# Moving three quarters of an attention output projection into the steps of the last attention group

## The chip, the cores and the metric

The kernel runs on one core of a Trainium2 chip. The metric is the time of one execution in microseconds (us), measured on the device; a kernel's time is the median of its runs. The engines are PE (TensorE, matrix products), ACT (ScalarE), DVE (VectorE), POOL (GpSimd) and SP, which here only starts DMA transfers. Each takes its instructions in program order, and waits between engines are semaphore counts.

## What is computed

A decoder trunk of two layers on 512 positions and a model width of 1024: sparse attention (NSA), a SwiGLU feed-forward (FFN), a Mamba-2 mixer, a second FFN. The part at issue is the end of the attention and the start of the first FFN:

```python
    gates = jax.nn.sigmoid(g.astype(jnp.float32)).reshape(B, S, G, HP, 3, 1)
    o = (gates[..., 0, :] * o_c + gates[..., 1, :] * o_s + gates[..., 2, :] * o_w).astype(h.dtype)
    return o.reshape(B, S, NSA_Q_WIDTH) @ w_out
...
        h = h + mix.astype(h.dtype)
        h = h + swiglu(rms_norm(h, ffn_norm_w[i]), ffn_w_gate[i], ffn_w_up[i], ffn_w_down[i]).astype(h.dtype)
```

## The kernel before

Activations are kept transposed: `xT` is 128 partitions x 8 tiles (`KT`) x 512 positions. Every dense product is done in three matmuls, because each fp32 operand is split into a rounded high part and a rest: high x high, high x rest, rest x high (`split_product`). Weights arrive in chunks of 1 MB (128 x 2048 floats) through a ring of two slots: SP loads chunk n into `wraw[n % 2]`, ACT copies it into `wh` (`split_hi`, 128x2048), DVE writes the rest into `wl` (`split_lo`), and PE multiplies. SP may load chunk n+2 once `lo_done` says that chunk n is split; `split_hi` of chunk n waits until PE has finished chunk n-2 (`products`, two counts for each chunk).

Attention is done in 4 groups of 4 heads, each group in 18 steps `k`. Each engine has its own program for a step, in this order:

- PE: for k = 8, 12, 16 first `pv` of a head (18 matmuls); then `qk(k)` (scores of a head h = k // 4 and a block of 128 queries i = k % 4, so that the width is (i+1) x 128), small steps for the compressed attention at k = 0, 1, 5, then `pT(k-2)` (2(i+1) transposes of the probabilities).
- DVE: `maxima(k)` of the scores, `normalize(k-1)` of the exponentials, compressed attention at k = 1 and 3, and at k = 14 `o_rest(0)`; the last, `o_rest(1)`, follows after step 17.
- ACT: `exps(k-1)`, `pT_copy(k-2)` from PSUM, and `o_copy`.

`maxima(k)` waits for `qk(k)`, `exps` for the maxima, `normalize` for the exponentials, `pT` for `normalize`, `pT_copy` for `pT`, and `pv` for the copies of four blocks. The first three groups also carry the q/k/v projection of the next group (`project`, 8 matmuls in each of the steps 0 to 11, all into PSUM bank 7, which ACT empties). They also split the next two weight chunks in steps 14 and 15. The last group carries nothing besides attention. Heads come out two at a time as one tile of `xo` (high) and `xol` (rest), 8 tiles in all; tiles 6 and 7 are those of the last group.

Then follows `residual("nsa_out")`: four chunks of the output weights, each of 256 columns by all 8 input tiles. PE makes 8 output tiles of 24 matmuls into banks 0 to 3 in turn. For each pair of tiles DVE adds the two banks to `xT` (loaded again from memory by ACT's queue) and makes `xl` (`x_lo`), and ACT makes the squares for the norm (`square`) and `xh` (`x_hi`), POOL adds the squares up. Three `split_hi`/`split_lo` go between the pairs. The FFN begins with `pe.wait_ge(evac, t0)`: all 8 tiles must have been added to `xT`. Its first chunk needs `xh` and `xl` tile by tile; between its two output tiles stand `column_sums`, for which POOL must be done.

Of the kernel before, what the change touches and what calls it, by code (L numbers as in the profile page):

```python
# [31 lines left out]
P = 128  # L32
# [48 lines left out]
def chunk_plan():  # L81

    at, n = {}, 0
    for name, count in (("kv_cmp", 2), ("gates", 1), ("qkv", 8), ("nsa_out", 4), ("up0", 2 * FT // 2),
                        ("down0", 12), ("xbc", 12), ("dt", 1), ("z", 8), ("ssm_out", 8),
                        ("up1", 2 * FT // 2), ("down1", 12)):
        at[name] = n
        n += count
    return at, n


CHUNK, NCHUNKS = chunk_plan()

EVAC, _t = {}, 0
for _name, _count in (("kv_cmp", 4), ("gates", 1), ("qkv", 16), ("nsa_out", 8), ("up0", FT), ("down0", 8),
# [8 lines left out]
def trunk(nc, wstream, xT_in, cols_in, rows_in, pos_in, cw1_in, cw2_in, ident_in, tri_in, cmask_in, out):  # L104
    with ExitStack() as ctx:
# [3 lines left out]
        def sem(name):  # L109
            return ctx.enter_context(nc.semaphore(name))  # L110


        class Region:
# [4 lines left out]
            def take(self, name, shape, dt=F32):  # L118
# [110 lines left out]
        a = Region(arena_at)  # L229
        yl = a.take("yl", [P, TT, 16, P], F32R)  # L230
        a = Region(act_at)
        yh = a.take("yh", [P, TT, 16, P], F32R)
        assert a.end <= res_at
        a = Region(scratch_at)
# [16 lines left out]
            sem, ("masks_cast", "square_sum_zeroed", "squares_done", "square_sum_done", "colsum_done",  # L251
                  "mean_square_done", "rms_rstd_done", "diag_done", "rstd_broadcast_done"))
        xh_done, xl_done, vz_zeroed, vz_done = map(sem, ("xh_done", "xl_done", "vz_zeroed", "vz_done"))
        gate_in, gate_done, hh_done, hl_done = map(sem, ("gate_normed", "gate_done", "hidden_hi_done", "hidden_lo_done"))
        vec, pool_self = map(sem, ("vector_step", "pool_step"))
        (mhalf_set, kvT, tb_act, tb_vec, tbT_done, rows_mm, rows_copied, hid_mm, hid_done, cmp_mm, kc_sq, kc_mean, kc_rstd, kcn_done, kcT, kc_hi, kc_padded, kc_staged,
# [41 lines left out]

        Q4 = "p (h d) -> p h d"

        RES = {"nsa_out": [8], "ssm_out": [8, 8], "down0": [8, 8, 6], "down1": [8, 8, 6]}
        NORM = {"nsa_out": 1, "down0": 2, "ssm_out": 3}

        EARLY = ("nsa_out", "down0")
        NORMCOL = [COL_MIX, COL_FFN, COL_MIX + KT, COL_FFN + KT]

        block = ctx.enter_context(nc.Block())
# [2 lines left out]
        @block.sync  # L310
        def _(sp):
            sp.dma_start(cols[:, :], cols_in).then_inc(cols_landed, 16)
            for k in range(4):
                sp.dma_start(xT[:, 2 * k:2 * k + 2, :], xT_in[:, 2 * k:2 * k + 2, :]).then_inc(x_landed[k], 16)
                if k == 0:
                    sp.dma_start(wraw[:, 0, :], wstream[0]).then_inc(landed[0], 16)
            sp.dma_start(wraw[:, 1, :], wstream[1]).then_inc(landed[1], 16)
            sp.dma_start(tri[:, :, :], tri_in).then_inc(params_landed, 16)
            sp.dma_start(ident[:, :], ident_in).then_inc(params_landed, 16)
            sp.dma_start(rows[:, :], rows_in).then_inc(params_landed, 16)  # L320
            sp.dma_start(posi[:, :], pos_in).then_inc(rest_landed, 16)
            sp.dma_start(cmask[:, :, :, :], cmask_in).then_inc(rest_landed, 16)
            sp.dma_start(cw1[:, :, :, :], cw1_in).then_inc(cw_landed, 16)
            sp.dma_start(cw2[:, :, :, :], cw2_in).then_inc(cw_landed, 16)
            with sp.Fori(1, NCHUNKS // 2) as i:
                for k in range(2):

                    sp.wait_ge(lo_done, 2 * i + (k - 1))
                    sp.dma_start(wraw[:, k, :], wstream[bass.ds(2 * i + k, 1)].rearrange("a p n -> p (a n)")
                                 ).then_inc(landed[k], 16)  # L330
            for t in range(KT):
                sp.wait_ge(evac, EVAC["down1"] + t + 1)
                sp.dma_start(out[:, t, :], xT[:, t, :]).then_inc(out_stored, 16)
            sp.wait_ge(out_stored, 16 * KT)
# [3 lines left out]
        def _(pe):  # L338
# [180 lines left out]
            def group(g, more):  # L519
# [68 lines left out]
                def project(part):  # L588
# [12 lines left out]
                    if third == 2:  # L601
                        ins.then_inc(products, 1)

                for k in range(18):
                    if k in (8, 12, 16):
                        pv((k - 8) // 4)
                    if k < 16:
                        qk(k)
                    if k == 0:
                        cmp_scoresT()  # L610
                    if k == 1:
                        cmp_scores()
                    if k == 5:
                        cmp_transposes()
                    if k >= 2:
                        pT(k - 2)
                    if more and k < 12:
                        project(k)
                    if more and k == 16:
                        pe.wait_ge(evac, g * 4 + (t0 + 4))  # L620
                        qk_transposes(g + 1, (0, 1, 2), lambda h: (h - 1) % 8)
                    if more and k == 17:
                        qk_transposes(g + 1, (3, 4), lambda h: h - 1)
                        pe.wait_ge(qkT_lo, g * 6 + 7)
                        qk_transposes(g + 1, (5,), lambda h: 7)
# [26 lines left out]
                pe.wait_ge(qkT_lo, g * 6 + 12)  # L652
            group(GROUPS - 1, False)
            pe.wait_ge(o_lo, 2 * GROUPS)
            residual("nsa_out", lambda kt: (xo[:, kt, :], xol[:, kt, :]))
            ffn("up0", "down0", 1)


# [135 lines left out]
        def _(act):  # L794
# [27 lines left out]
            def residual(name):  # L822
                ks, n0, t0 = RES[name], CHUNK[name], EVAC[name]
                per = 2 * len(ks)
                ahead = name in ("nsa_out", "ssm_out")

                def turn(i, shift):

                    for p in range(2):
                        for q in range(len(ks)):  # L830
                            n = n0 + p * len(ks) + q + 1 + shift * per
                            if n < NCHUNKS and not ahead:
                                split_hi(n, i, per)
                            if ahead and q < len(ks) - 1:
                                split_hi(n + 1)
                        if name in NORM:
                            for m in range(2):
                                t = 2 * p + m + 4 * shift
                                square(t, NORM[name], i, 4, t0)
                                if name in EARLY:  # L840
                                    x_hi(NORM[name], t if i is None else i * 4 + t)
                        if ahead and n + 1 <= n0 + 2 * per:
                            split_hi(n + 1)
                if n0 + 2 * per < NCHUNKS and not ahead:
                    with act.Fori(0, 2) as i:
                        turn(i, 0)
                else:
                    turn(None, 0)
                    turn(None, 1)
                if name in NORM and name not in EARLY:  # L850
                    for kt in range(KT):
                        x_hi(NORM[name], kt)

# [85 lines left out]
            def group(g, more):  # L939
# [18 lines left out]
                def o_copy(pr):  # L958
                    act.wait_ge(pv_done, g * 4 + 2 * (pr + 1))
                    A(xo[:, bass.ds(g * 2 + pr, 1), :].rearrange("p a n -> p (a n)"), ps[:, 6, :], ACT.Copy  # L960
                      ).then_inc(o_hi, 1)

                for k in range(18):
# [23 lines left out]
                    if more and k in (14, 15):  # L987
                        act.wait_ge(products, g * 4 + 2 * (n0 + 4))
                        split_hi(n0 + 4 + k - 14, g, 2)
                o_copy(1)  # L990

            transposed_hi(0, (0, 1, 2), lambda h: h)
# [4 lines left out]
            A(Bc[:, 0, :], ps[:, 6, 3 * P:4 * P], ACT.Copy).then_inc(kc_hi, 1)  # L997
            with act.Fori(0, GROUPS - 1) as g:
                group(g, True)
            group(GROUPS - 1, False)  # L1000
            act.wait_ge(o_lo, 2 * GROUPS)
            act.dma_start(xT[:, :, :], xT_in).then_inc(x_again, 16)
            residual("nsa_out")
            ffn("up0", "down0", 1)


# [106 lines left out]
        def _(dve):  # L1113
# [35 lines left out]
            def residual(name):  # L1149
                ks, n0, t0 = RES[name], CHUNK[name], EVAC[name]  # L1150
                per = 2 * len(ks)
                ahead = name in ("nsa_out", "ssm_out")

                def turn(i, shift):
                    for p in range(2):
                        for q in range(len(ks)):
                            n = n0 + p * len(ks) + q + 1 + shift * per
                            if n < NCHUNKS and not ahead:
                                split_lo(n, i, per)
                            if ahead and q < len(ks) - 1:  # L1160
                                split_lo(n + 1)
# [9 lines left out]
                                x_lo(NORM[name], t if i is None else i * 4 + t)  # L1171
                        if ahead and n + 1 <= n0 + 2 * per:
                            split_lo(n + 1)
                if n0 + 2 * per < NCHUNKS and not ahead:
# [131 lines left out]
            def group(g, more):  # L1306
# [56 lines left out]
                for k in range(18):  # L1363
# [21 lines left out]
                        transposed_lo(g + 1, (3, 4, 5), lambda h: h - 1 if h < 5 else 7)  # L1385
                    if more and k in (14, 15):
                        split_lo(n0 + 4 + k - 14, g, 2)
                o_rest(1)

            split_lo(5)  # L1390
# [37 lines left out]
                group(g, True)  # L1428
            V.leave(GROUPS - 1, DVE_GROUP_STEPS)
            group(GROUPS - 1, False)  # L1430
            dve.wait_ge(x_again, 16)
            residual("nsa_out")
            ffn("up0", "down0", 1)


# [370 lines left out]
```

## Time and profile before

| what | value |
|---|---|
| median of 3 runs | 1648.72 us (1648.58 to 1653.01) |
| span of the profiled execution | 1649.7 us |
| PE busy | 1561.1 us, 95% of the span |
| DVE busy | 867.8 us, 53% |
| ACT busy | 631.6 us, 38% |
| POOL busy | 258.2 us, 16% |
| mean granted PE clock | 0.975 of 2.4 GHz |

The span goes from the first to the last instruction of one profiled execution. The profiled execution is not among the three timed runs and has no time of its own beside its span; the span is 1.0 us above the median of the runs. Busy time counts matrix products from their start to a modelled end, so two that follow each other overlap: a product of 128x512 is shown as 0.39 us long, but the next starts 0.23 us after it. Start to start is therefore what a product costs.

### The profile page before, as it was taken

How to read it: one execution, taken by the hardware profiler on the slowest of the kernel's cores; microseconds unless marked ns; L12 is line 12 of the kernel's file. 1: busy time of each engine (PE TensorE's matmuls, PEld its weight loads, DVE VectorE, ACT ScalarE, POOL GpSimd, SP SyncE). 2: the span in 40 equal slices, each digit the busy share in tenths (PEclk: the TensorE clock that was granted, in tenths of full speed). 3: DMA queues.
4: the chain of work that ended last, by engine and by line, in shares of the span. 5: the costliest groups of instructions: out<-in, count | busy, mean ns of one | idle time of the engine just before them, and what ended most of it. 6: DMA issues, size and time to landing. Idle time of an engine off the chain costs nothing.

```text
span 1649.7 us, 19940 instructions
## 1 busy us (share of the span) xinstructions
PE 1561.1 (95%) x7085; PEld 1223.5 (74%) x7085; DVE 867.8 (53%) x1265; ACT 631.6 (38%) x895; POOL 258.2 (16%) x288
## 2 busy tenths in 40 slices
PE   5989999988999999999999999998799999999999
PEld 4766666654778888878888877666587788887887
DVE  4555767574444444432377766778732544444222
ACT  4444555554334433422233353444222434433111
POOL 4133131400200000000000015666311000000000
PEclk9989999989999999999999999999799999999999
DMA  7200101010222222223222221110022222222222
GB/s 302 77 26 1 52 0 51 0 51 1 102 91 87 102 102 102 102 80 124 102 77 103 85 94 51 52 51 27 24 77 103 77 102 80 98 102 102 103 102 76
DMA packets 19196, 129.44 MB, mean 78 GB/s; under 512 B 2256, under 2 KB 2896, under 8 KB 4560
## 3 DMA queue, kind: packets, MB, share of 16 engines
q1 hardware_dynamic: 19008, 126.75, 21.4%
q10 hardware_dynamic: 144, 2.10, 0.4%
q8 instruction: 28, 0.46, 0.1%
q14 instruction: 16, 0.13, 0.0%
HBM read 126.74 MB, written 2.10 MB: 78 GB/s over the span
## 4 chain that ended last, share of the span: by engine, by line
PE 83%; issue 5%; DVE 5%; POOL 5%; ACT 2%; DVEq 0%; POOLq 0%; ACTq 0%
PE ps L343 21%; PE ps L344 21%; PE ps L345 21%; PE ps L582 4%; PE ps L599 3%; PE ps L747 2%; PE ps L565 2%; POOL Lx L1697 2%; PE ps L579 1%; PE ps L530 1%; POOL sqacc L1623 1%; DVE Pm L1355 1%; PE ps L719 1%; PE ps L531 1%; PE ps L777 1%
## 5 line engine op out<-in xcount | busy, mean ns | idle before, releaser
L1125 DVE TENSOR_TENSOR wl<-wraw,wh 128x2048 fp32r<-128x2048 f32 x112 | 264.7, 2364 | 273.9 <-ACT wh L802 273.8
L343 PE MATMUL ps<-xh,wh 128*128 128x512 f32 (+2 forms) x912 | 358.9, 393 | 6.1 <-DVE xl L1135 3.4
L345 PE MATMUL ps<-xh,wl 128*128 128x512 f32 (+2 forms) x912 | 355.9, 390 | 0.0
L344 PE MATMUL ps<-xl,wh 128*128 128x512 f32 (+2 forms) x912 | 355.9, 390 | 0.0
L802 ACT ACTIVATE wh<-wraw 128x2048 fp32r<-128x2048 f32 x112 | 213.9, 1910 | 186.3 <-PE ps L345 176.6
L343 PEld LDWEIGHTS ps<-xh,wh 128*128 128x128 f32 (+2 forms) x912 | 170.4, 187 | 44.3 <-issue 4.5
L345 PEld LDWEIGHTS ps<-xh,wl 128*128 128x128 f32 (+2 forms) x912 | 170.5, 187 | 37.2
L344 PEld LDWEIGHTS ps<-xl,wh 128*128 128x128 f32 (+2 forms) x912 | 170.6, 187 | 36.8 <-issue 0.7
L343 PE MATMUL ps<-hh,wh 128*128 128x512 f32 x352 | 138.0, 392 | 4.0 <-DVE hid L1205 4.0
L345 PE MATMUL ps<-hh,wl 128*128 128x512 f32 x352 | 137.6, 391 | 0.0
L344 PE MATMUL ps<-hl,wh 128*128 128x512 f32 x352 | 137.6, 391 | 0.0
L1623 POOL TENSOR_TENSOR sqacc<-sqacc,sq 128x512 f32<-128x512 f32 x32 | 44.2, 1381 | 482.0 <-ACT sq L811 481.0
L864 ACT ACTIVATE hh<-hid 128x512 f32 x44 | 27.8, 632 | 188.4 <-DVE hid L1205 188.4
L1342 DVE TENSOR_REDUCE sm<-ps 128x2 f32<-128x256 f32 (+1 forms) x64 | 52.5, 821 | 70.1 <-PE ps L532 70.1
L343 PEld LDWEIGHTS ps<-hh,wh 128*128 128x128 f32 x352 | 66.4, 189 | 18.7 <-DVE hid L1205 4.9
L955 ACT ACTIVATE PT<-ps 128x256 f32<-128x256 f32 (+1 forms) x64 | 45.1, 704 | 91.5 <-PE ps L565 91.5
L344 PEld LDWEIGHTS ps<-hl,wh 128*128 128x128 f32 x352 | 66.5, 189 | 13.8
L345 PEld LDWEIGHTS ps<-hh,wl 128*128 128x128 f32 x352 | 66.5, 189 | 13.8
L947 ACT ACTIVATE Pm<-ps,sm 128x128 f32<-128x128 f32 (+3 forms) x128 | 66.3, 527 | 23.6 <-DVE sm L1344 23.4
L582 PE MATMUL ps<-PT,vst 128*64 128x512 f32 (+3 forms) x256 | 74.0, 443 | 0.0
L582 PEld LDWEIGHTS ps<-PT,vst 128*64 128x64 f32 x256 | 35.2, 141 | 48.7 <-issue 43.6
L1168 DVE TENSOR_TENSOR xT<-ps,xT 128x512 f32<-128x512 f32 (+1 forms) x32 | 22.1, 690 | 85.7 <-PE ps L345 77.9
(257 smaller groups left out, 2560.1 us busy)
## 6 DMA issues: line engine op xcount, KB each, us to landing
wraw<-wstream SPq DMA_DIRECT2D x112, 1024.0 KB, 4.8
cw<-cw_in SPq DMA_DIRECT2D x1, 4096.0 KB, 18.3
xT<-xT_in SPq DMA_DIRECT2D x4, 512.0 KB, 9.0
xT<-xT_in ACTq DMA_DIRECT2D x1, 2048.0 KB, 7.8
out<-xT SPq DMA_DIRECT2D x8, 256.0 KB, 6.6
rows<-rows_in SPq DMA_DIRECT2D x1, 276.0 KB, 11.1
tri<-tri_in SPq DMA_DIRECT2D x1, 192.0 KB, 9.7
cmask<-cmask_in SPq DMA_DIRECT2D x1, 128.0 KB, 10.5
```

The lines of the kernel that those rows point to most:

```text
L343: mm(o, wa[0], xa[0], start=start, stop=False)
L344: mm(o, wa[0], xa[1], start=False, stop=False)
L345: return mm(o, wa[1], xa[0], start=False, stop=stop)
L565: ins = pe.transpose(ps[:, 4 + b, j * P:(j + 1) * P], Pm[:, s % 2, b, j * P:(j + 1) * P], ident[:, :])
L582: ins = mm(o[:, j * P:], vst[:, j, b, :], PT[:, h % 2, b, j, j * P:], start=False, stop=b == 1 and j == TT - 1)
L599: ins = mm(ps[:, 7, :], (xh, xl, xh)[pss][:, kt, t], (wh, wh, wl)[pss][:, slot, w], start=m == 0, stop=m == 23)
L802: A(wh[:, n % 2, :], wraw[:, n % 2, :], ACT.Copy).then_inc(hi_done, 1)
L947: A(Pm[:, s % 2, b, 0:w], ps[:, 2 * (s % 2) + b, 0:w], ACT.Exp, bias=sm[:, 4, m + 2 + b:m + 3 + b], scale=SCALE, accum_out=sm[:, 4, m + 4 ...
L955: A(PT[:, h % 2, :, 0:i + 1, i * P:(i + 1) * P], ps[:, 4:6, 0:(i + 1) * P].rearrange("p b (j q) -> p b j q", q=P), ACT.Copy).then_inc(pT_d ...
L1125: TTo(wl[:, s, :], wraw[:, s, :], wh[:, s, :].bitcast(F32), ALU.subtract).then_inc(lo_done, 1)
L1342: step(dve.tensor_reduce(sm[:, 4, m:m + 2], ps[:, 2 * (s % 2):2 * (s % 2) + 2, 0:(i + 1) * P], AX, ALU.max))
L1623: TTo(sqacc[:, :], sqacc[:, :], sq[:, mt % 2, :], ALU.add).then_inc(acc_done, 1)
```

## The change

The output projection is cut in two by input tiles. The 6 input tiles that groups 0 to 2 leave (`EARLY_KT = 6`) are multiplied inside the last group: each step k = 0 to 15 gets `out_early(k)`, half of an output tile t = k // 2, which is 9 matmuls into PSUM bank 7, after `pT(k-2)`. DVE adds bank 7 into `part[t]`, a copy of `xT_in` loaded by ACT's queue before the group, at the end of its step k = 2(t+1). PE waits for that addition (`part_done`) before it begins the next tile. The splits of the chunks 2, 3 and 4 of the projection (counted from `NS` = 0) are put into ACT's and DVE's steps 4, 8 and 12, on DVE ahead of the addition. The last two input tiles (6 and 7) of all four chunks are gathered by one more DMA into a fifth ring chunk, and multiplied after the group: 8 output tiles of 6 matmuls, then the additions, `square`, `x_hi` and `x_lo` per pair as before. The first FFN chunk is split by ACT and DVE between the group and these additions.

```diff
-        RES = {"nsa_out": [8], "ssm_out": [8, 8], "down0": [8, 8, 6], "down1": [8, 8, 6]}
+        NS = CHUNK["nsa_out"]
+        EARLY_KT = 6
+        RES = {"ssm_out": [8, 8], "down0": [8, 8, 6], "down1": [8, 8, 6]}
...
+            sp.wait_ge(lo_done, NS + 3)
+            sp.dma_start(wraw[:, (NS + 4) % 2, :].rearrange("p (c n) -> p c n", c=4),
+                         wstream[NS:NS + 4, :, EARLY_KT * 256:].rearrange("c p n -> p c n")
+                         ).then_inc(landed[(NS + 4) % 2], 16)
...
+                def out_early(k):
+
+                    t, half = divmod(k, 2)
+                    c, m = divmod(t, 2)
+                    if k == 0:
+                        pe.wait_ge(o_lo, EARLY_KT)
+                    if half == 0:
+                        pe.wait_ge(lo_done, NS + c + 1)
+                        after(pe, part_done, t)
+                    for kt in range(3 * half, 3 * half + 3):
+                        w = slice(kt * 256 + m * P, kt * 256 + (m + 1) * P)
+                        s = (NS + c) % 2
+                        ins = split_product(ps[:, 7, :], (wh[:, s, w], wl[:, s, w]), (xo[:, kt, :], xol[:, kt, :]),
+                                            kt == 0, kt == EARLY_KT - 1)
+                    if half:
+                        ins.then_inc(products, 1)
...
                 for k in range(18):
                     if k in (8, 12, 16):
                         pv((k - 8) // 4)
...
                     if more and k < 12:
                         project(k)
+                    if not more and k < 16:
+                        out_early(k)
...
             group(GROUPS - 1, False)
             pe.wait_ge(o_lo, 2 * GROUPS)
-            residual("nsa_out", lambda kt: (xo[:, kt, :], xol[:, kt, :]))
+            pe.wait_ge(lo_done, NS + 5)
+            for t in range(KT):
+                pe.wait_ge(evac, EVAC["nsa_out"] + t - 3)
+                s = (NS + 4) % 2
+                for kt in range(EARLY_KT, KT):
+                    w0 = t // 2 * 512 + (kt - EARLY_KT) * 256 + t % 2 * P
+                    ins = split_product(ps[:, t % 4, :], (wh[:, s, w0:w0 + P], wl[:, s, w0:w0 + P]),
+                                        (xo[:, kt, :], xol[:, kt, :]), kt == EARLY_KT, kt == KT - 1)
+                if t < KT - 1:
+                    ins.then_inc(out_mm, 1)
+                else:
+                    ins.then_inc(products, 2)
```

On ACT, the first lines stand at the end of a step of `group`:

```diff
+                    if not more and k in (4, 8, 12):
+                        split_hi(NS + 1 + k // 4)
...
+            act.dma_start(part[:, :, :], xT_in).then_inc(x_again, 16)
             group(GROUPS - 1, False)
-            act.wait_ge(o_lo, 2 * GROUPS)
-            act.dma_start(xT[:, :, :], xT_in).then_inc(x_again, 16)
-            residual("nsa_out")
+            split_hi(NS + 5)
+            for t in range(KT):
+                square(t, 1, None, 0, EVAC["nsa_out"])
+                x_hi(1, t)
```

On DVE, the first lines stand at the end of a step of `group`, after `maxima(k)` and `normalize(k-1)`:

```diff
+                    if not more and k in (4, 8, 12):
+                        split_lo(NS + 1 + k // 4)
+                    if not more and k % 2 == 0 and k:
+                        t = k // 2 - 1
+                        if t == 0:
+                            dve.wait_ge(x_again, 16)
+                        dve.wait_ge(products, 2 * NS + t + 1)
+                        TTo(part[:, t, :], ps[:, 7, :], part[:, t, :], ALU.add).then_inc(part_done, 1)
                 o_rest(1)
...
             group(GROUPS - 1, False)
-            dve.wait_ge(x_again, 16)
-            residual("nsa_out")
+            split_lo(NS + 5)
+            for p in range(KT // 2):
+                for t in (2 * p, 2 * p + 1):
+                    if t < KT - 1:
+                        dve.wait_ge(out_mm, t + 1)
+                    else:
+                        dve.wait_ge(products, 2 * (NS + 5))
+                    TTo(xT[:, t, :], ps[:, t % 4, :], part[:, t, :], ALU.add).then_inc(evac, 1)
+                for t in (2 * p, 2 * p + 1):
+                    x_lo(1, t)
+            mean_square(1)
+            diagonal(1)
             ffn("up0", "down0", 1)
```

What is left out here are the chunk numbers of the ring, which has one chunk more than the stream, and SP's loop around the gathered chunk.

## Rows read from the trace of the kernel before

**Rows 1.** the page, part 4: shares of the chain that ended last
```profile
PE 83%; issue 5%; DVE 5%; POOL 5%; ACT 2%; DVEq 0%; POOLq 0%; ACTq 0%
```

**Rows 2.** busy time of each engine by stretch: PE, PEld, DVE, ACT, POOL, clock
```profile
268.24:347.87 79.63, 74.94 (x386) 51.14 (x385) 52.73 (x133) 43.24 (x102) 21.16 (x36) 0.98 0.07 26
347.87:412.30 64.43, 54.39 (x265) 34.36 (x264) 36.56 (x111) 30.77 (x85) 0.00 (x0) 0.92 0.00 1
...
413.97:459.99 46.02, 45.24 (x193) 36.10 (x193) 18.00 (x18) 14.17 (x18) 9.30 (x8) 1.00 0.32 114
459.99:466.34 6.35, 6.35 (x32) 5.42 (x33) 1.87 (x2) 5.70 (x5) 1.29 (x1) 1.00 0.00 0
```

**Rows 3.** waits of PE, 347.87 to 414: total us, times, longest us
```profile
PE ps L565 <- DVE Pm L1355: 4.4, 5, 2.4
...
PE ps L565 <- ACT PT L955: 1.6, 3, 1.0
PE ps L579 <- ACT PT L955: 1.1, 1, 1.1
PE ps L541 <- DVE xol L1360: 1.0, 1, 1.0
```

**Rows 4.** timeline of PE in a group that projects: start, us, instruction
```profile
277.79 0.47 PE L599 MATMUL ps<-wh,xl 128*128 128x512 f32 x1
...
279.73 0.40 PE L530 MATMUL ps<-kB,qA 128*128 128x512 f32 x1
```

**Rows 5.** timeline of PE in the last group, steps 12 to 14
```profile
390.11 0.83 PE L565 MATMUL ps<-ident,Pm 128*128 128x128 f32 x6
390.69 0.36 PE L530 MATMUL ps<-kB,qA 128*128 128x256 f32 x1
...
393.94 0.23 PE L532 MATMUL ps<-negmask_bf,ident_bf 128*128 128x128 bf16 x1
```

**Rows 6.** timeline of DVE, step 14 of the last group
```profile
394.21 0.96 DVE L1342 TENSOR_REDUCE sm<-ps 128x2 f32<-128x768 f32 x1 [0.51 <-PE ps L532]
...
395.76 0.17 DVE L1351 RECIPROCAL sm<-sm 128x2 f32<-128x2 f32 x1 [0.39 <-ACT Pm L947]
...
396.69 0.69 DVE L1360 TENSOR_TENSOR xol<-ps,xo 128x512 fp32r<-128x512 f32 x1
```

**Rows 7.** timeline of ACT, step 12 of the last group
```profile
390.97 0.81 ACT L955 ACTIVATE PT<-ps 128x768 f32<-128x768 f32 x1 [4.25 <-PE ps L565]
391.68 0.36 ACT L947 ACTIVATE Pm<-ps,sm 128x128 f32<-128x128 f32 x1
```

**Rows 8.** timeline of ACT, output projection, tiles 5 and 6
```profile
449.87 1.90 ACT L802 ACTIVATE wh<-wraw 128x2048 fp32r<-128x2048 f32 x1
454.74 0.63 ACT L811 ACTIVATE sq<-xT 128x512 f32<-128x512 f32 x1 [2.96 <-DVE xT L1168]
455.27 0.71 ACT L816 ACTIVATE xh<-xT,cols 128x512 fp32r<-128x512 f32 x1
```

**Rows 9.** timeline of DVE, output projection, tiles 5 to 7
```profile
451.81 2.29 DVE L1125 TENSOR_TENSOR wl<-wraw,wh 128x2048 fp32r<-128x2048 f32 x1 [0.53 <-ACT wh L802]
454.02 0.68 DVE L1168 TENSOR_TENSOR xT<-ps,xT 128x512 f32<-128x512 f32 x1
459.24 0.69 DVE L1168 TENSOR_TENSOR xT<-ps,xT 128x512 f32<-128x512 f32 x1 [4.54 <-PE ps L345]
459.85 0.74 DVE L1135 SCALAR_TENSOR_TENSOR xl<-xT,cols,xh 128x512 fp32r<-128x512 f32 x1
```

**Rows 10.** windows as in rows 2, around idle stretches of PE
```profile
1054.50:1057.80 3.30, 3.30 (x10) 2.53 (x9) 1.95 (x4) 0.72 (x2) 1.50 (x3) 0.50 0.80 283
1100.20:1102.90 2.70, 0.00 (x0) 0.00 (x0) 2.70 (x2) 1.23 (x1) 2.70 (x2) 0.89 0.00 0
1102.90:1108.60 5.70, 5.70 (x13) 4.46 (x14) 2.59 (x5) 0.90 (x3) 3.90 (x5) 0.50 0.53 184
358.20:368.40 10.20, 9.34 (x41) 7.95 (x42) 7.72 (x23) 5.41 (x15) 0.00 (x0) 0.50 0.00 0
```

More of the change, by code:

```diff
@@ L83, in chunk_plan @@
     at, n = {}, 0
-    for name, count in (("kv_cmp", 2), ("gates", 1), ("qkv", 8), ("nsa_out", 4), ("up0", 2 * FT // 2),
+    for name, count in (("kv_cmp", 2), ("gates", 1), ("qkv", 8), ("nsa_out", 5), ("up0", 2 * FT // 2),
                         ("down0", 12), ("xbc", 12), ("dt", 1), ("z", 8), ("ssm_out", 8),
@@ L89, in chunk_plan @@
     return at, n
-CHUNK, NCHUNKS = chunk_plan()
+CHUNK, NRING = chunk_plan()
+NCHUNKS = NRING - 1
 EVAC, _t = {}, 0
@@ L231, in trunk @@
         a = Region(act_at)
+        part = a.take("part", [P, KT, SEQ])
+        a = Region(act_at)
         yh = a.take("yh", [P, TT, 16, P], F32R)
@@ L253, in trunk @@
         xh_done, xl_done, vz_zeroed, vz_done = map(sem, ("xh_done", "xl_done", "vz_zeroed", "vz_done"))
+        part_done, out_mm = sem("out_part_added"), sem("out_tile_done")
         gate_in, gate_done, hh_done, hl_done = map(sem, ("gate_normed", "gate_done", "hidden_hi_done", "hidden_lo_done"))
@@ L299, in trunk @@
         Q4 = "p (h d) -> p h d"
-        RES = {"nsa_out": [8], "ssm_out": [8, 8], "down0": [8, 8, 6], "down1": [8, 8, 6]}
-        NORM = {"nsa_out": 1, "down0": 2, "ssm_out": 3}
-        EARLY = ("nsa_out", "down0")
+        NS = CHUNK["nsa_out"]
+        EARLY_KT = 6
+        RES = {"ssm_out": [8, 8], "down0": [8, 8, 6], "down1": [8, 8, 6]}
+        NORM = {"down0": 2, "ssm_out": 3}
+        EARLY = ("down0",)
         NORMCOL = [COL_MIX, COL_FFN, COL_MIX + KT, COL_FFN + KT]
@@ L324, in _, with chunk_pair @@
             sp.dma_start(cw2[:, :, :, :], cw2_in).then_inc(cw_landed, 16)
-            with sp.Fori(1, NCHUNKS // 2) as i:
+            def chunk_pair(i, shift):
                 for k in range(2):
                     sp.wait_ge(lo_done, 2 * i + (k - 1))
-                    sp.dma_start(wraw[:, k, :], wstream[bass.ds(2 * i + k, 1)].rearrange("a p n -> p (a n)")
+                    sp.dma_start(wraw[:, k, :], wstream[bass.ds(2 * i + (k - shift), 1)].rearrange("a p n -> p (a n)")
                                  ).then_inc(landed[k], 16)
+            with sp.Fori(1, (NS + 4) // 2) as i:
+                chunk_pair(i, 0)
+            for k in range(NS + 3 - (NS + 3) % 2, NS + 4):
+                sp.wait_ge(lo_done, k - 1)
+                sp.dma_start(wraw[:, k % 2, :], wstream[k]).then_inc(landed[k % 2], 16)
+            sp.wait_ge(lo_done, NS + 3)
+            sp.dma_start(wraw[:, (NS + 4) % 2, :].rearrange("p (c n) -> p c n", c=4),
+                         wstream[NS:NS + 4, :, EARLY_KT * 256:].rearrange("c p n -> p c n")
+                         ).then_inc(landed[(NS + 4) % 2], 16)
+            with sp.Fori((NS + 5) // 2, NRING // 2) as i:
+                chunk_pair(i, 1)
+            sp.wait_ge(lo_done, NRING - 2)
+            sp.dma_start(wraw[:, (NRING - 1) % 2, :], wstream[NCHUNKS - 1]).then_inc(landed[(NRING - 1) % 2], 16)
             for t in range(KT):
@@ L824, in residual @@
                 per = 2 * len(ks)
-                ahead = name in ("nsa_out", "ssm_out")
+                ahead = name == "ssm_out"
                 def turn(i, shift):
@@ L831, in turn @@
                             n = n0 + p * len(ks) + q + 1 + shift * per
-                            if n < NCHUNKS and not ahead:
+                            if n < NRING and not ahead:
                                 split_hi(n, i, per)
@@ L843, in turn @@
                             split_hi(n + 1)
-                if n0 + 2 * per < NCHUNKS and not ahead:
+                if n0 + 2 * per < NRING and not ahead:
                     with act.Fori(0, 2) as i:
@@ L1151, in residual @@
                 per = 2 * len(ks)
-                ahead = name in ("nsa_out", "ssm_out")
+                ahead = name == "ssm_out"
                 def turn(i, shift):
@@ L1157, in turn @@
                             n = n0 + p * len(ks) + q + 1 + shift * per
-                            if n < NCHUNKS and not ahead:
+                            if n < NRING and not ahead:
                                 split_lo(n, i, per)
@@ L1173, in turn @@
                             split_lo(n + 1)
-                if n0 + 2 * per < NCHUNKS and not ahead:
+                if n0 + 2 * per < NRING and not ahead:
                     with dve.Fori(0, 2) as i:
```

## The prediction

> **What bounds the kernel now.** I read the shares of the chain that ended last first [rows 1]: 83% of it is PE, so the kernel as a whole is a string of matrix products, and work moved within PE gains nothing unless it lands where PE would have waited. Next come the busy times by stretch [rows 2]. The reader is to compare two things there: the last attention group (64.43 us, PE busy 54.39, so 10.04 of waiting, at a mean clock of 0.92) and the output projection behind it (46.02 us, PE busy 45.24, hardly any waiting). The projection's 192 products cost 45.24 / 193 = 0.234 us each. The group has holes, the projection has none: moving products from the second to the first is the only way in which this edit can pay, and at most about 10 us of holes are there. A group that does carry extra products is in the same view: group 2, 79.63 us with 96 projection products. Then I read the waits of PE in the last group [rows 3], and the timelines of the single steps [rows 4 to 9], because the question is what the moved products wait for.
>
> **What the change takes away behind the group.** Count from the end of the last `pv` at 412.30. Before, the last of the eight additions to `xT` began at 459.24 [rows 9], 46.9 us later, and the FFN's second tile began at 466.34 [rows 2], 7.1 us after that addition; the 7.1 stay, since PE's wait for all eight tiles, the 24 products and `column_sums` are unchanged. After the change PE has only 48 products there, 48 x 0.234 = 11.2 us. But DVE does not start with the additions. ACT copies the last head pair (0.53 us start to start, by the `square` of the same size [rows 8]) and runs `split_hi` of the first FFN chunk; DVE's `split_lo` starts 1.94 us after it (449.87 to 451.81), and the next addition 2.21 us later (451.81 to 454.02) [rows 8, 9]. So the first addition begins 0.5 + 1.9 + 2.2 = 4.7 us after `pv`. Then the pairs are a chain between two engines: addition to `square` 0.72 (454.02 to 454.74), `square` and `x_hi` 1.24 for each of two tiles, the second `x_lo` 0.7, less 0.1 of overlap, 3.8 us for a pair [rows 8, 9]. PE's 1.4 us a tile hides under 1.9 us a tile. The last addition begins at 4.7 + 3 x 3.8 + 0.6 = 16.7 us. **Gain: 46.9 - 16.7 = 30.2 us.** POOL's sums (9.30 us for eight [rows 2]) and the split of the second FFN chunk keep their place relative to the last addition, and cost nothing while `column_sums` and the second tile cover them as before.
>
> **What it adds to the group.** Eight products of a projection part cost 1.94 us start to start (277.79 to 279.73) [rows 4]; with a ninth 2.17, and 16 parts make **+34.7 us**. They fill old waits: of the 10.04 us, 3.1 stay (1.0 at the compressed scores and 1.0 + 1.1 in the last two steps, which get no products) [rows 3], so **-6.9**. Each of some 11 filled waits also had the end of a product in front of it that the next one could not overlap: six transposes are shown as 0.83 us but cost 0.58 (390.11 to 390.69) [rows 5], about 0.2 each, **-2.4**. From 358.2 to 368.4 the granted clock was 0.50, the 1.2 GHz level, after PE had sat idle for 2.4 us [rows 3, 10]; without that loss the 9.34 busy us there would be about 6.4 (my estimate: a third, between the nearly half that 512-column products lose and the little that short ones lose), **-2.9**, to be given back below.
>
> **The new waits.** PE may not begin tile t before DVE has added tile t-1 out of bank 7. DVE does that at the end of its own step k = 2t, and that step begins with `maxima(k)`, which waits for `qk(k)` of the same step. So the addition can't be early: it always comes a whole DVE step after `qk(k)`, and PE has only a few transposes to do in between. It is the same bank and the same order in every even step from 2 to 14: seven waits.
>
> Steps 4, 8 and 12, with a split ahead of the addition. From the start of `pT(k-2)` to ACT's copy of it 0.86 us (390.11 to 390.97), the copy 0.71 (to 391.68), `split_hi` to `split_lo` 1.94, `split_lo` 2.21, the addition 0.69, back to PE 0.05: 6.5 us, less the 0.58 of the transposes, is 5.9 us of wait [rows 5, 7 to 9]. Three of them: **+17.7**.
>
> Steps 2, 6 and 10. From the last product of `qk(k)` to `maxima` 0.27 us (393.94 to 394.21), maxima and normalize 396.69 - 394.21 - 0.39 of waiting = 2.09, the addition 0.69, back 0.05: 3.1, less 0.2 for two transposes, 2.9 us [rows 5, 6]. Step 14 has `o_rest(0)` before the addition, 0.6 more. **+12.2**. What queues behind PE's wait is the whole of PE: the next `qk`, hence the next maxima, exponentials and normalization. The sum for the group is 34.7 - 6.9 - 2.4 - 2.9 + 17.7 + 12.2 = **+52.4 us**, and with the 30.2 back, **+22.2 us**.
>
> **The clock.** After an idle 2.70 us (1100.20 to 1102.90) 13 products took 5.70 us at 0.50, 0.44 us each and not 0.234; another low stretch lasted 3.3 us, and the one after the 2.4 us idle 10.2 [rows 3, 10]. A low stretch costs 1 - 0.234 / 0.44 = 0.47 of its length in dense products, 1.6 us for the 3.3 and 2.7 for the 5.7. All seven new waits are longer than 2.4. I take the middle, 2.1 us for each: **+14.7 us**. Bounds: none, if such waits do not bring the clock down, and 5.0 us for each if it stays down until the next wait (between two waits PE has 4.3 us of products, which lose 0.88 of that, and about 3 of short ones, by the 3.8 us from 390.11 to 393.94 [rows 5] with a wait in them; these lose under half): 35 us. The middle is nearer to the lower end because two of the three stretches ended within 6 us.
>
> The Trainium skill, "TensorE: Matmul & The Clock Gate", section on HAM oscillation, puts the penalty at half of the throttled time whatever runs in it. By that rule and the mean of the three stretches, 6.4 us, seven waits would cost 22 us and the kernel would take 1693. The row from 358.2 to 368.4 is against the full half, since its short products and transposes lose less.
>
> **Edits that I cost at nothing.** The gathered chunk may be loaded once the third chunk is split in step 4, and is needed in step 12, some 50 us later by this sum; uncovered it would cost its landing. The load of `part` starts before the group and is first needed in step 2, about 10 us later, when PE has done steps 0 and 1 with 4.3 us of new products in them; were it later, step 2's wait would grow by the rest. ACT issues it before it has anything else to do in the group.
>
> **Sum.** 22.2 + 14.7 = 36.9 us. The profiled execution's span of 1649.7 would become 1686.6; it lay 1.0 above the median of the runs, so the median goes from 1648.7 to 1685.6.
>
> **Rivals.** (a) The other side: DVE's addition is not on PE's path, because the order of DVE's step leaves it time before PE asks. Then no new wait and no clock loss: 34.7 - 12.2 - 30.2 = -7.7, 1641.0 us. It decides if all new waits and clock losses together stay under 7.7 us, and they would have to stay under 2.8 for a gain of 0.3%. For it: in group 2 the evacuation of the same bank hardly stops PE, which is busy 74.94 of 79.63 us [rows 2]. Against it: there ACT does it, and nothing of the step's own `qk` stands in front. (b) Only the steps with a split wait; plain additions come in time: -7.7 + 17.7 + 3 x 2.1 = +16.3, 1665.0. Against it: `maxima(k)` in front of the addition. (c) All the waits, and the clock stays at 2.4 GHz: +22.2, 1670.9. For it: the last group has a mean clock of 0.92 with four waits of about 1 us and one of 2.4 in it, so not every wait brings it down [rows 2, 3]; against it, the new waits are longer than the one that did [rows 10]. (d) The clock stays down between the waits: 22.2 + 35, 1705.9. For it: the 10.2 us stretch, whose mix of `qk` and transposes is that of this group. (e) It does nothing: a wash between waits and gains by chance, within 5 us of before.
>
> **How the numbers follow.** Forecast (1677 to 1695) 0.50; (b) and (c) together 0.22; (d) 0.13; slower through some other mixture 0.07; (e) 0.03; (a) 0.05. The range from 1662 to 1702 takes in (b), (c) and the nearer part of (d), and leaves out some 2 in 10. A measurement of this kernel can tell about 0.3%, 5 us, from no change; slower by more than that 0.92, within it 0.03, faster 0.05.
>
> **What the changed profile would show.** In the waits of PE the line of `out_early` appears, released by DVE's addition into `part`, seven times, three near 5.9 us and four near 3. The last group lasts about 64.4 + 52.4 + 14.7 = 131 us; its granted clock falls under 0.9. From the last `pv` to the last addition to `xT` it is about 17 us, with DVE and ACT in turn and PE idle in part. If PE doesn't wait for `part`, (a) is right and my reading of DVE's order is wrong; if it does but the low clock stretches are short, (c); if the clock is at 0.50 for most of the group, (d). The prediction is also wrong if ACT is late with `split_hi`, which makes the three long waits longer than 6.

## The result and the profile after

The changed kernel takes 1686.7 us (median of 4 runs, 1684.54 to 1687.64) against 1650.51 us for the kernel before, run beside it (4 runs, 1648.58 to 1653.01). The ratio is 1.022, 95% interval 1.0207 to 1.0232: slower by 2.2%, some 36 us. The forecast was 1685.6.

The span of the profiled execution is 1682.7 us. The chain that ended last (part 4 of the page) has lost two points of PE and won one of DVE, against [rows 1]:

```profile
PE 81%; DVE 6%; issue 5%; POOL 5%; ACT 2%; DVEq 0%; ACTq 0%; POOLq 0%
```

The waits of PE in the stretch of the last group and of what is left of the output projection (total us, times, longest us), against [rows 3]:

```profile
PE ps L362 <- DVE part L1448: 28.7, 7, 6.0
PE ps L362 <- DVE xol L1413: 1.4, 1, 1.4
PE ps L598 <- ACT PT L1004: 1.1, 1, 1.1
PE ps L560 <- DVE xol L1413: 1.0, 1, 1.0
PE ps L584 <- ACT PT L1004: 1.0, 1, 1.0
```

The first line is new: seven times PE stood still until DVE had added bank 7 into `part`, 28.7 us in all. The three old waits at the ends of the group stand as they were, and `normalize` and the exponentials no longer stop PE at all. The busy times by stretch (PE, PEld, DVE, ACT, POOL, clock), against [rows 2]: the group, the eight short tiles, PE's idle time before the FFN, and the FFN's first tile:

```profile
347.32:470.73 123.41, 91.55 (x409) 63.56 (x408) 48.49 (x122) 36.61 (x89) 0.00 (x0) 0.88 0.12 43
470.73:484.20 13.47, 11.76 (x48) 8.88 (x48) 10.30 (x10) 7.16 (x10) 5.59 (x5) 1.00 0.24 79
484.20:491.53 7.33, 0.00 (x0) 0.00 (x1) 6.56 (x7) 2.99 (x6) 3.41 (x3) 0.71 0.00 0
491.53:499.92 8.39, 8.39 (x25) 6.66 (x25) 3.03 (x2) 6.23 (x7) 2.82 (x2) 0.64 0.00 0
```

The group went from 64.45 us (347.87 to the last copy of `xo` at 412.32) to 123.41, +59.0. From there to `column_sums` it was 53.2 us before (412.32 to 465.54) and is 29.2 now (470.73 to 499.92), -24.0. The two together are 117.67 us before and 152.60 after: **+34.9 us**. After `column_sums` the two spans have 1184.2 and 1182.8 us left, so nothing else moved by more than 1.5 us. These two stretches are used below for every kernel, because they repeat: kernels with the same code in the group differ there by under 0.05 us, while whole runs of one kernel spread over 1 to 9 us.

**A long wait, step 4.** PE, then ACT, then DVE, each from its own timeline:

```profile
368.39 0.82 PE L584 MATMUL ps<-ident,Pm 128*128 128x128 f32 x6
375.19 0.76 PE L362 MATMUL ps<-xo,wh 128*128 128x512 f32 x1 [5.97 <-DVE part L1448]
375.75 0.63 PE L363 MATMUL ps<-xol,wh 128*128 128x512 f32 x1
```

```profile
369.26 0.81 ACT L1004 ACTIVATE PT<-ps 128x768 f32<-128x768 f32 x1 [0.84 <-PE ps L584]
369.96 1.90 ACT L851 ACTIVATE wh<-wraw 128x2048 fp32r<-128x2048 f32 x1
```

```profile
370.44 0.42 DVE L1395 TENSOR_REDUCE sm<-ps 128x2 f32<-128x256 f32 x1
...
372.16 2.28 DVE L1178 TENSOR_TENSOR wl<-wraw,wh 128x2048 fp32r<-128x2048 f32 x1
374.36 0.68 DVE L1448 TENSOR_TENSOR part<-ps,part 128x512 f32<-128x512 f32 x1
```

PE has done its six transposes at 369.2 and then waits 5.97 us. ACT copies them (369.26), then does `split_hi` (369.96 to 371.86). DVE is never idle in between: it has the compressed attention of step 3 to finish before its `maxima(4)` can begin at 370.44, is through with `normalize` at 372.16, does `split_lo`, and only then, at 374.36, the addition that PE needs. So in step 4 it is DVE's own backlog that PE waits for. In the steps 8 and 12 nothing is left over on DVE, and there `split_lo` waits for ACT's `split_hi`, as in the row of step 8:

```profile
402.07 2.29 DVE L1178 TENSOR_TENSOR wl<-wraw,wh 128x2048 fp32r<-128x2048 f32 x1 [1.50 <-ACT wh L851]
```

Back in step 4, the product that then starts (375.19) is 0.76 us long, and the next comes 0.56 us after it, not 0.23: the granted clock is down, at 0.50 (the row from 375.19 below).

**The tail.** Of DVE's pairs of tiles (start, length) the first, and POOL's first pair of additions of squares:

```profile
473.16 2.29 DVE L1178 TENSOR_TENSOR wl<-wraw,wh 128x2048 fp32r<-128x2048 f32 x1 [1.11 <-ACT wh L851]
475.37 1.28 DVE L1499 TENSOR_TENSOR xT<-ps,part 128x512 f32<-128x512 f32 x2
477.36 3.06 DVE L1188 SCALAR_TENSOR_TENSOR xl<-xT,cols,xh 128x512 fp32r<-128x512 f32 x2 [0.72 <-ACT xh L865]
480.35 1.27 DVE L1499 TENSOR_TENSOR xT<-ps,part 128x512 f32<-128x512 f32 x2
```

```profile
476.88 3.00 POOL L1694 TENSOR_TENSOR sqacc<-sqacc,sq 128x512 f32<-128x512 f32 x2 [4.24 <-ACT sq L860]
```

The two `x_lo` take 3.06 us together, 1.5 each, where [rows 9] has one of 0.74, and a pair takes 4.98 us (475.37 to 480.35). POOL works from 476.88 to 479.88, over the whole of them.

### The profile page after: what moved, and what is told of

It is laid out like the page before. It is cut to its first block, busy times and chain, and to the rows that moved or that the text cites. A ratio compares the mean times of both kernels' runs of the same rounds, so it can differ in the third digit from the quotient of the medians.

```text
span 1682.7 us, 19934 instructions
## 1 busy us (share of the span) xinstructions
PE 1567.9 (93%) x7085; PEld 1227.3 (73%) x7085; DVE 880.4 (52%) x1274; ACT 633.1 (38%) x896; POOL 258.9 (15%) x288
## 4 chain that ended last, share of the span: by engine, by line
PE 81%; DVE 6%; issue 5%; POOL 5%; ACT 2%; DVEq 0%; ACTq 0%; POOLq 0%
PE ps L362 21%; PE ps L363 21%; PE ps L364 21%; PE ps L601 4%; PE ps L618 3%; PE ps L584 2%; PE ps L796 2%; POOL Lx L1768 2%; PE ps L598 1%; PE ps L549 1%; DVE wl L1178 1%; PE ps L550 1%; POOL sqacc L1694 1%; DVE Pm L1408 1%; DVE sm L1395 1%
## 5 line engine op out<-in xcount | busy, mean ns | idle before, releaser
L909 ACT ACTIVATE gate<-gate 128x512 f32<-128x512 f32 x44 | 27.7, 632 | 104.2 <-DVE gate L1251 104.2
```

## The experiments

The kernels e1 to e5 differ from the changed kernel by the edit shown; e6 to e8 build on e2. The table has the median, the ratio to the kernel before with its interval where there is more than one run, and from the profiled execution the group (start of `qk(0)` to the last copy of `xo`) and the tail (from there to `column_sums`), in us.

| kernel | median | ratio (95%) | PE's waits for `part` | group | tail | group + tail |
|---|---|---|---|---|---|---|
| before | 1649 to 1650.5 | 1 | none | 64.45 | 53.22 | 117.67 |
| the change | 1686.7 | 1.022 (1.0207 to 1.0232) | 28.7 | 123.41 | 29.19 | 152.60 |
| e1, addition before the split | 1675.69 | 1.0164 (1.0147 to 1.0181) | 19.0 | 116.78 | 29.18 | 145.96 |
| e2, addition first | 1651.58 | 1.0013 (1.0001 to 1.0025) | 3.4 | 90.04 | 28.88 | 118.92 |
| e3, POOL's sums narrow | 1680.21 (1 run) | | 28.7 | 123.43 | 25.77 | 149.20 |
| e4, splits narrow | 1677.77 (1 run) | | 19.2 | 116.66 | 29.16 | 145.82 |
| e5, waits filled | 1675.55 | 1.0152 (1.0134 to 1.0169) | 4.9 | 114.23 | 28.74 | 142.97 |
| e6, e2 and the early split | 1648.38 | 0.9989 (0.9976 to 1.0002) | 3.4 | 90.05 | 26.95 | 117.00 |
| e7, e6 and a new tail order | 1644.56 | 0.9969 (0.9958 to 0.998) | 3.4 | 90.06 | 22.83 | 112.89 |
| e8, e7 and a filled gap | 1643.24 | 0.9953 (0.9937 to 0.9969) | 3.4 | 90.08 | 22.30 | 112.38 |

### e1: the addition ahead of the split

```diff
+                    if not more and k % 2 == 0 and k:
...
                     if not more and k in (4, 8, 12):
                         split_lo(NS + 1 + k // 4)
-                    if not more and k % 2 == 0 and k:
```

The lines of the addition under this condition are the same ones, moved up.

> DVE's addition into part is put ahead of its split_lo in the steps 4, 8 and 12 (order alone, the same work). If the wait of PE is DVE's own order: the three long waits fall from 5.7 to 6.0 us to 2.1 to 3, the seven waits together from 28.7 to about 19 us, and with fewer low clock stretches after them the kernel takes 10 to 15 us less than the change, 1672 to 1677. If the split itself is what PE needs (its weights), nothing changes, 1686.

Measured: 1675.69 us, and the waits fell by the 9.7 us that were expected:

```profile
PE ps L362 <- DVE part L1446: 19.0, 7, 3.8
```

The split is part of the long waits because it stood ahead of the addition. Single waits came out beside the expected 2.1 to 3 us: step 4 kept 3.77 us, for DVE's backlog of step 3 is still ahead of the addition, and the steps 8 and 12 fell to 1.93. But the group shrank by only 6.6 us (123.41 to 116.78), and its clock did not rise:

```profile
343.83:460.61 116.78, 94.68 (x409) 65.85 (x408) 48.54 (x122) 36.61 (x89) 0.00 (x0) 0.87 0.13 45
```

PE is busy 94.68 us there, 3.1 more than in the change, with the same instructions. The part of the expectation that fewer low stretches come with shorter waits is wrong: here the granted clock was 0.50 after all seven waits, of 1.93 to 3.77 us, in stretches that add up to 27.0 us of PE's work, and in the change after five of seven, 20.1 us. The span of its profiled execution is 10.0 us shorter than the change's (1672.7), of which 3.5 lie ahead of the group, in code that is the same in both (`qk(0)` starts at 343.83 and not at 347.32).

### e2: the addition as the first thing in DVE's step

```diff
                 for k in range(18):
+                    if not more and k % 2 == 0 and k:
...
                     if k < 16:
                         maxima(k)
```

The condition's lines, the addition, move ahead of `maxima` unchanged.

> DVE's addition is the first thing in its step, ahead of maxima(k). If maxima(k), which waits for this step's qk, is what makes the addition late: the seven waits fall from 28.7 us to under 4 together, the granted clock of the group rises to over 0.97, and the kernel takes about 34 us less than the change, 1653, near the kernel before. What stays is the slower tail behind the group. If bank 7 or the addition itself were the limit, the waits would stay above 1 us each and the time above 1670.

Measured: 1651.58 us. The waits for `part` are down to 3.4 us, of which 2.1 is one wait in step 4, where DVE is held by the compressed attention of step 3:

```profile
PE ps L362 <- DVE xT L1499: 7.7, 2, 7.4
PE ps L362 <- DVE part L1422: 3.4, 4, 2.1
```

```profile
347.51:437.55 90.04, 83.49 (x409) 58.13 (x408) 48.44 (x122) 36.84 (x88) 0.00 (x0) 0.98 0.16 59
```

The group takes 90.04 us at a clock of 0.98. The same work, one statement moved: 33.4 us. This is the condition of rival (a), "DVE's addition is not on PE's path", made nearly true, and it settles that the cause of the waits is the place of the addition behind `maxima(k)` and `normalize(k-1)`, not bank 7 as such: bank 7 is still the only one. What stays is the wait in the first line above, on `xT`: PE waits 7.4 us for the last addition to `xT`.

### e4: the splits narrowed

`split_hi` and `split_lo` of the steps 4, 8 and 12 work on 8 of 2048 columns, so most of three weight chunks is not refreshed.

```diff
-                        split_lo(NS + 1 + k // 4)
+                        split_lo(NS + 1 + k // 4, w=8)
```

> The three splits inside the last group are done on 8 of 2048 columns by ACT and DVE (so the output projection is wrong), all waits and orders kept. If the long waits are the short ones plus the splits: 5.7 to 6.0 becomes 2.1 to 3, the seven together about 19 us, the time 1670 to 1677, as when the addition goes ahead of the split. If it comes out much faster than that, the splits also cost ACT's and DVE's other work something.

Measured: 1677.77 us in one run; waits 19.2 us, group 116.66. Both agree with e1 to 0.2 us; the median lies 0.8 us above the expected range, in a single run. So the splits cost the group their share of the long waits and nothing else; ACT and DVE had room for them.

### e5: useless products inside the waits

```diff
+                    if not more and k % 2 == 0 and 2 <= k < 16:
+                        pe.wait_ge(expd, g * 32 + 2 * k)
+                        for n in range(22 if k % 4 == 0 else 9):
+                            mm(ps[:, 2 * ((k + 1) % 2), :], wh[:, (NS + k // 4) % 2, 0:P], xo[:, 0, :], start=True, stop=True)
                     if not more and k < 16:
                         out_early(k)
```

> The changed kernel with useless 128x512 products added on PE inside its own waits: 22 ahead of each of the three long waits and 9 ahead of each of the four short ones, 102 in all (24 us), into the score banks that the next qk overwrites; the moment at which part is ready stays the same. If the low clock after the waits costs about 8 us in the group: the granted clock stays at 2.4 GHz there and the kernel takes 6 to 9 us less than the change, 1678 to 1681, though PE does 24 us more. If the clock costs nothing: the same time as the change, 1686, or more.

Measured: 1675.55 us against 1686.7, with 102 products more; that is 11 us less, where 6 to 9 were expected. The group (columns as above):

```profile
346.62:460.85 114.23, 106.24 (x511) 75.30 (x510) 48.50 (x122) 36.62 (x89) 0.00 (x0) 1.00 0.13 47
```

It has 511 products where the change has 409, and takes 114.23 us, 9.2 less, at a clock of 1.00 and not 0.88. The waits that are left (4.9 us) and the 102 x 0.234 = 23.9 us of filling make 28.8, the same 28.7 as before: nothing became ready earlier. So 9.2 us of the change's loss in the group is PE's clock. The other 2 us lie outside the group and are within the spread of whole runs.

### e3: POOL's additions narrowed

Ahead of the first FFN POOL adds up 8 of the 512 columns of the squares.

```diff
+                    w = 8 if L == 1 else SEQ
-                    TTo(sqacc[:, :], sqacc[:, :], sq[:, mt % 2, :], ALU.add).then_inc(acc_done, 1)
+                    TTo(sqacc[:, 0:w], sqacc[:, 0:w], sq[:, mt % 2, 0:w], ALU.add).then_inc(acc_done, 1)
```

> POOL's eight additions of squares before the first FFN are done on 8 of 512 columns (so the norm is wrong from there). If x_lo takes 1.5 us and not 0.7 because POOL works at the same time: x_lo falls to about 0.7, a pair of tiles from 4.9 to 3.8 us, and the last addition to xT comes about 3.4 us earlier; the kernel gains 3 to 4 us, a little more if PE's idle stretch there gets too short to bring the clock down. If x_lo is slow for another reason, nothing changes.

Measured: 1680.21 us in one run, and DVE's first pair:

```profile
474.40 1.28 DVE L1499 TENSOR_TENSOR xT<-ps,part 128x512 f32<-128x512 f32 x2
476.40 0.75 DVE L1188 SCALAR_TENSOR_TENSOR xl<-xT,cols,xh 128x512 fp32r<-128x512 f32 x1 [0.72 <-ACT xh L865]
477.54 0.75 DVE L1188 SCALAR_TENSOR_TENSOR xl<-xT,cols,xh 128x512 fp32r<-128x512 f32 x1 [0.38 <-ACT xh L865]
478.20 1.28 DVE L1499 TENSOR_TENSOR xT<-ps,part 128x512 f32<-128x512 f32 x2
```

`x_lo` is back at 0.75 us and the pair at 3.80 us (474.40 to 478.20), which is the 3.8 us of the prediction. The tail is 3.4 us shorter, so POOL's additions do slow `x_lo`. (That this one run is 6.5 us below the change is more than the tail explains.) POOL's own additions take 1.50 us each in the change and 1.29 before; no experiment isolates that.

### e6, e7, e8: the tail

e6 is e2 with the split of the first FFN chunk in step 17 of the group (on both engines), e7 adds a new order on DVE, e8 adds products on PE.

```diff
+                    if not more and k == 17:
+                        split_lo(NS + 5)
...
-            split_lo(NS + 5)
-            for p in range(KT // 2):
...
+            for t in range(KT):
...
+                TTo(xT[:, t, :], ps[:, t % 4, :], part[:, t, :], ALU.add).then_inc(evac, 1)
+                if t:
+                    x_lo(1, t - 1)
+            x_lo(1, KT - 1)
```

```diff
+            for n in range(18):
+                mm(ps[:, 4, :], xo[:, 0, 0:P], xo[:, 0, :], start=True, stop=True)
             ffn("up0", "down0", 1)
```

In e7's loop the line left out is the wait for tile t, as before.

> The kernel whose addition stands first, and the split of the first FFN chunk moved from behind the group into its step 17, where ACT and DVE sit idle for 5 and 13 us. If the split in front of the tail's additions is on the path: the first addition begins when the first tile is done, about 3.3 us after the last pv and not 4.7, and the kernel gains about 1.4 us, 1650. If PE's tiles are the limit of the tail anyway, nothing changes.

> The kernel of the early split, and in the tail DVE adds tile t+1 before it makes xl of tile t, so that it no longer waits for ACT. If the alternation of DVE and ACT is part of the tail's 4.9 us a pair: DVE works without a gap, 0.64 + 1.5 us a tile, 4.3 us a pair, the last addition comes 1 to 2.5 us earlier, and the kernel takes 1647 to 1649, 0 to 0.2% less than the kernel before. If DVE under POOL's load is the whole of it, the gain is under 1 us.

> The kernel of the new tail order, and 18 useless products (4.2 us) on PE between its last tile and its wait for the last addition. If the low clock at the start of the FFN costs 2.5 to 3 us: that stretch runs at 2.4 GHz and the kernel takes 1644 to 1646. If the idle time in the new order is already too short to bring the clock down, nothing changes; if the products are longer than the idle time, it loses up to 1 us.

Measured: e6 took 1.9 us off the tail (1.4 expected), e7 another 4.1, more than expected. Its DVE rows:

```profile
445.44 0.68 DVE L1500 TENSOR_TENSOR xT<-ps,part 128x512 f32<-128x512 f32 x1
446.05 1.18 DVE L1189 SCALAR_TENSOR_TENSOR xl<-xT,cols,xh 128x512 fp32r<-128x512 f32 x1
447.15 0.68 DVE L1500 TENSOR_TENSOR xT<-ps,part 128x512 f32<-128x512 f32 x1
```

A tile takes 1.71 us (445.44 to 447.15), and `x_lo` 1.18, not 1.5: with an addition out of PSUM between two `x_lo`, DVE and POOL collide for less of the time. That explanation is argued, not isolated; the shorter `x_lo` was not foreseen. A pair of tiles took about 4.95 us in the change, of which 0.71 was DVE waiting for ACT's `x_hi`; that wait and some 0.7 us of the two `x_lo` are gone. e8 gained 0.5 us of the 2.5 to 3 expected. In e7, PE's idle time before the FFN and then the FFN's first tile:

```profile
446.00:449.90 3.90, 1.17 (x5) 0.65 (x4) 3.90 (x6) 2.84 (x5) 3.42 (x3) 1.00 0.00 0
449.90:456.78 6.88, 6.88 (x25) 5.47 (x23) 2.14 (x2) 5.36 (x5) 1.61 (x2) 0.75 0.00 0
```

and in e8 the tile alone:

```profile
454.80:461.57 6.77, 6.77 (x32) 5.55 (x31) 2.63 (x3) 5.73 (x5) 2.09 (x2) 1.00 0.00 0
```

The clock rises from 0.75 to 1.00 and the tile's products take 5.5 us (456.08 to 461.57) and not 7.2 (449.56 to 456.78). But the idle time in e7 was only 2.7 us, and 4.25 us of useless products kept PE from its start by 1.2 us. e7 and e8 are both faster than the kernel before, by 0.3% and 0.5%; in group and tail by 4.8 and 5.3 us of 117.67. Between e7 and e8 the medians decide nothing (e8's six runs go from 1640.61 to 1646.38, around e7's 1644.56), so the 0.5 us rests on the stretches alone.

## Why the prediction came out right, and which of its terms were off

The sign, the mechanism and the sum were right: +36.9 us forecast, +36 measured in the medians and +34.9 in the two stretches. That the total is nearer than its terms is luck: the loss from the clock was put 5.5 us too high and the gain behind the group 6.2 us too high, and the two misses nearly cancelled.

- **The new waits.** 17.7 us for the three long ones, measured 5.97 + 5.72 + 5.72 = 17.4; 12.2 for the four short ones, measured 2.83 + 2.63 + 2.63 + 3.22 = 11.3. That they come from DVE's order is shown by e2, and the part of the split by e1 and e4. One agreement is luck: the 5.9 us was worked out along ACT's copy and `split_hi`. The steps 8 and 12 go that way (5.72), but step 4 comes to 5.97 by DVE's compressed attention of step 3, which the prediction had not counted; it also holds `maxima(2)` in step 2. Rivals (a) and (b) are out: the short waits are there too.
- **The work and the old holes.** 34.7 - 6.9 - 2.4 - 2.9 = 22.5 us was forecast. Measured it is 59.0 - 28.7 - 9.2 = 21.1. In e2, where hardly any new wait is left, the group took 25.6 us more than before, with 3.4 us of waits, so 22.2. The holes that could be filled were worth about 12 us, as forecast; the 34.7 us of products did not fit into them. The -2.9 for the low clock that the group had before was too small. It rests on the reading that short products and transposes lose little at the low clock, and the trace before has the same work at both levels: eight transposes take 1.62 us at the low one and 0.85 at the full one, half a `qk` of three blocks 0.88 and 0.47.

```profile
364.85 1.97 PE L565 MATMUL ps<-ident,Pm 128*128 128x128 f32 x8 [0.60 <-DVE Pm L1355]
366.47 0.67 PE L530 MATMUL ps<-kB,qA 128*128 128x384 f32 x1
...
392.18 1.09 PE L565 MATMUL ps<-ident,Pm 128*128 128x128 f32 x8 [0.57 <-DVE Pm L1355]
393.03 0.42 PE L530 MATMUL ps<-kB,qA 128*128 128x384 f32 x1
```

They lose nearly half, as the long products do, so this row is not against the full half, as the prediction says. By 0.47 of the 9.34 us the term is -4.4 (an estimate), and the four terms then give 21.0, beside the 21.1 measured.
- **The clock in the group.** The step that failed in size: "I take the middle, 2.1 us for each: +14.7 us". e5 shows 9.2 us, 1.3 for each wait. Two of the seven waits, both of 2.63 us, did not bring the clock down at all; the rows of the change around the first of them are

```profile
384.00:386.67 2.67, 0.04 (x1) 0.03 (x1) 2.42 (x7) 1.62 (x5) 0.00 (x0) 1.00 0.00 0
386.67:399.40 12.73, 12.72 (x58) 7.87 (x58) 2.96 (x9) 2.05 (x5) 0.00 (x0) 1.00 0.00 0
```

and after the other five it stayed down for 2.9 to 5.8 us of PE's work:

```profile
361.00:364.30 3.30, 3.30 (x9) 2.64 (x8) 0.00 (x0) 0.00 (x0) 0.00 (x0) 0.50 0.00 0
375.19:378.05 2.86, 2.86 (x7) 2.28 (x8) 0.00 (x0) 0.00 (x0) 0.00 (x0) 0.50 0.71 256
405.11:408.75 3.64, 3.64 (x9) 2.86 (x10) 0.00 (x0) 0.00 (x0) 0.00 (x0) 0.50 0.82 288
434.97:439.50 4.53, 4.53 (x13) 3.58 (x13) 0.00 (x0) 0.00 (x0) 0.00 (x0) 0.50 0.64 231
447.37:453.15 5.78, 5.78 (x14) 4.01 (x14) 0.00 (x0) 0.00 (x0) 0.00 (x0) 0.50 0.01 3
```

These are 20.1 us at 1.2 GHz, and 0.47 of that, the prediction's own loss per us, is 9.4: the price per us was right, and the number and length of the stretches were not. No run shows what sets their length. Rivals (c) and (d), no clock loss and a clock that stays down, are both out by e5 and these rows. The Trainium skill, "TensorE: Matmul & The Clock Gate", section "HAM oscillation — how this bites in real kernels", counts half of the throttled time as lost. The trace agrees: half of the 20.1 us is 10.1, beside 9.2 measured. The 22 us of the prediction came from its lengths, seven stretches of 6.4 us.
- **The gain behind the group.** The step that failed: "the second `x_lo` 0.7 ... 3.8 us for a pair". A pair takes 4.98 us, because both `x_lo` run against POOL's additions (1.5 us each); e3 gives 3.80 without them. The last addition to `xT` began 20.1 us after the last `pv` (490.81 - 470.73, from DVE's rows), not 16.7. I took 0.74 us from the one `x_lo` that ran before POOL had started; in the kernel before, the next `x_lo` of that timeline ran beside POOL's addition and took 1.27:

```profile
461.24 1.27 DVE L1135 SCALAR_TENSOR_TENSOR xl<-xT,cols,xh 128x512 fp32r<-128x512 f32 x1 [0.65 <-ACT xh L816]
```

```profile
460.68 1.29 POOL L1623 TENSOR_TENSOR sqacc<-sqacc,sq 128x512 f32<-128x512 f32 x1 [3.86 <-ACT sq L811]
```

- **"The 7.1 stay".** They didn't: PE had stood idle 7.33 us, the clock was down, and the FFN's first tile took 8.39 us, against 5.5 in e8. From the last addition to `column_sums` it was 9.1 us (490.81 to 499.92), and 6.3 before. Together with the item above the gain was 24.0 us, not 30.2.
- **The edits costed at nothing.** They cost nothing here: in step 12 `split_hi` starts as soon as ACT's copy is done (430.00), so the gathered chunk had landed, and in step 2 DVE goes from `normalize` to the addition (359.62) without a gap, so `part` had.

The sum of the misses is -1.4 (work) - 5.5 (clock in the group) - 1.2 (waits) + 6.2 (tail) = -1.9 us, from 36.9 to 35.0. The price of rival (a) would have missed by more: e2 comes to +1.3 us in the two stretches and not -7.7, for its tail is slow in the same way and 3.4 us of waits are left.

The idea behind the edit does pay, but little: with the addition ahead, the split out of the tail and DVE's order changed, e7 is 0.3% faster than the kernel before. Group and tail have a floor in PE's work: the 44.9 us of projection products were never removed, only about 12 us of holes could be filled, and some 7 us of them are given back in waits of the tail and of step 4.

## What to carry to other kernels

When work of one engine is interleaved into another stage with a single buffer between producer and consumer, look where in the consumer's step the drain stands and what it waits for: a drain placed behind something that waits for the same step of the producer is late by a whole consumer step, here seven times out of seven. Put the drain first in the step; here that one move was worth 33 us. Before you move products into holes, add up the holes: what is moved beyond them only changes place, and a chain that the moved products had covered (additions, squares, splits) comes out into the open.

## What the runs showed of the hardware that was not expected

- A DVE operation with both inputs in SBUF (`x_lo`, 128x512) takes 0.75 us with POOL's additions cut to 8 columns (e3) and 1.5 us while POOL adds two 128x512 tiles; the addition out of PSUM (0.64 us start to start) is hardly touched. The Trainium skill, "SBUF — State Buffer", section "Who interferes with whom", says that a DVE instruction with two SBUF inputs contends with a GpSimd instruction that reads SBUF; the trace agrees, and in e7, with a DVE operation out of PSUM between every two of them, they take 1.18 us.
- PE did 102 products more and the kernel was 11 us faster in the medians, 9.2 us in the group (e5): after idle times of 2.8 us and more, products of 0.234 us cost 0.43 to 0.44 us for 2.7 to about 6 us. The length of an idle time alone does not tell whether the clock falls: after two of 2.63 us in the change the granted clock stayed at 1.00, while in e1 two of the same 2.63 us were followed by products at 0.62 and 0.59 (382.06 to 386.00 and 409.34 to 413.00), and after one of 1.93 us it was 0.50 from 398.70 to 402.05.
